# The token mixers of a hybrid diffusion trunk: linear attention laid between the projection's pages, and the other three mixers run for both streams in lockstep

## What is computed

```
h = RMSNorm(x) * (1 + scale1) + shift1
gq, gk, gv, gog, glr_f, glr_b, mcq, mckv, mkr, rq, rk, rv, rg, aq, ak, av = split(h @ w_in)   # 1024 x 2752
A = head_rms(bidir_recurrence(gq, gk, gv, log_sigmoid(glr @ gate_w + gate_b) / 16)) * silu(gog)
B = dense_attention(q from rms(mcq) @ w_q_up, k and v from rms(mckv) @ w_kv_up and mkr)
C = head_rms(bidir_recurrence(rq, rk, rv, fixed decay per head)) * silu(rg)
D = windowed attention of aq over ak, av with a sink logit
x = x + gate1 * concat(A, B, C, D) @ w_out
x = x + gate2 * FFN(RMSNorm(x) * (1 + scale2) + shift2)   # dense in layer 0, 2 of 8 experts in layer 1
```

## Time and profile before

| | us |
|---|---|
| median of 3 runs (lowest, highest) | 1899.84 (1897.28, 1901.28) |
| the profiled execution | 1889.91 |
| its span, first to last instruction | 1888.1 |
| TensorE busy | 1710.1, 91% |
| VectorE busy | 308.6, 16% |
| ScalarE busy | 233.8, 12% |
| GpSimd busy | 91.9, 5% |

### The profile page before, as it was taken

How to read it: one execution, slowest core, us unless ns; L and a number is a source line. 1 busy time by engine, 2 the same in 40 slices (tenths; PEclk the granted TensorE clock), 3 DMA queues, 4 the chain that set the end, 5 groups by cost and what they waited for, 6 DMA issues and landing times.

```text
span 1888.1 us, 42448 instructions
## 1 busy us (share of the span) xinstructions
PE 1710.1 (91%) x19946; PEld 1085.6 (57%) x19947; DVE 308.6 (16%) x731; ACT 233.8 (12%) x588; POOL 91.9 (5%) x150
## 2 busy tenths in 40 slices
PE   4996778999998976787999999999999999999995
PEld 1874354777767743545555565555655555555553
DVE  0105241000012042404001011010010100101102
ACT  1212221100002122112001010010010100101001
POOL 4022000200000030000000000000000000000000
PEclk7997778999998987577999999999999999999998
DMA  9753642444452545013898998999989999899880
GB/s 347 223 184 138 245 134 89 136 135 156 154 170 72 164 180 201 1 67 145 323 386 325 391 386 324 386 341 371 385 330 384 361 355 386 322 386 390 327 338 25
DMA packets 210447, 479.72 MB, mean 254 GB/s; under 512 B 8726, under 2 KB 54454, under 8 KB 203990
## 3 DMA queue, kind: packets, MB, share of 16 engines
q1 hardware_dynamic: 206876, 469.32, 68.1%
q0 software_dynamic: 3392, 7.63, 1.3%
HBM read 475.05 MB, written 1.87 MB: 253 GB/s over the span
## 4 chain that ended last, share of the span: by engine, by line
PE 88%; DVE 6%; ACT 3%; issue 2%; DMA 1%; SPq 0%; POOL 0%; DVEq 0%; POOLq 0%; ACTq 0%
PE ps L962 31%; PE ps L982 15%; PE ps L869 8%; PE ps L684 8%; PE ps L877 4%; PE ps L859 3%; PE ps L632 2%; PE ps L932 2%; PE ps L939 2%; PE ps L969 1%; PE ps L845 1%; DVE scratch L1423 1%; PE ps L826 1%; PE ps L706 1%; DMA arena<-in_w_mod 1%
## 5 line engine op out<-in xcount | busy, mean ns | idle before, releaser
L962 PE MATMUL ps<-arena,scratch 128*32 128x256 f32 x10752 | 605.4, 380 | 0.7 <-ACT scratch L1264 0.7
L962 PEld LDWEIGHTS ps<-arena,scratch 128*32 128x32 f32 x10752 | 342.5, 110 | 240.0 <-issue 21.5
L982 PE MATMUL ps<-arena,scratch 128*32 128x256 f32 x5376 | 300.5, 379 | 5.0 <-ACT scratch L1112 5.0
L982 PEld LDWEIGHTS ps<-arena,scratch 128*32 128x32 f32 x5376 | 174.0, 110 | 120.8 <-ACT scratch L1112 6.9
L1605 DVE TENSOR_TENSOR scratch<-scratch,ps 128x128 f32<-128x128 f32 x168 | 48.4, 288 | 782.6 <-ACT scratch L1273 782.6
L869 PE MATMUL ps<-hT,arena 128*128 128x256 f32 x704 | 157.1, 382 | 3.0 <-issue 3.0
L684 PE MATMUL ps<-arena,hT 128*128 128x256 f32 (+1 forms) x704 | 152.4, 380 | 6.2 <-issue 6.2
L869 PEld LDWEIGHTS ps<-hT,arena 128*128 128x128 f32 x704 | 134.9, 192 | 30.5 <-issue 13.0
L684 PEld LDWEIGHTS ps<-arena,hT 128*128 128x128 f32 x704 | 134.4, 193 | 24.4 <-issue 6.9
L1273 ACT ACTIVATE scratch<-ps 128x128 f32<-128x128 f32 x168 | 46.6, 277 | 801.9 <-PE ps L962 801.9
L877 PE MATMUL ps<-arena,scratch 128*128 128x512 f32 x176 | 79.0, 592 | 0.0
(11 more groups left out here) (296 smaller groups left out, 1022.6 us busy)
## 6 DMA issues: line engine op xcount, KB each, us to landing
arena<-in_moe_w_gate SPq DMA_DIRECT2D x112, 1024.0 KB, 8.3
arena<-in_moe_w_up SPq DMA_DIRECT2D x112, 1024.0 KB, 10.5
arena<-in_moe_w_down SPq DMA_DIRECT2D x112, 1024.0 KB, 13.8
arena<-in_w_mod SPq DMA_DIRECT2D x48, 1024.0 KB, 5.2
arena<-in_w_in SPq DMA_DIRECT2D x20, 1024.0 KB, 7.9
arena<-in_ffn_w_gate SPq DMA_DIRECT2D x11, 1024.0 KB, 5.5
arena<-in_ffn_w_up SPq DMA_DIRECT2D x11, 1024.0 KB, 8.0
arena<-in_ffn_w_down SPq DMA_DIRECT2D x11, 1024.0 KB, 5.1
```

What stands on the lines that cost most here:

```text
L962: ins = mm(ps[32 * g:32 * g + 32, 4 + i % 3, 0:256], e_h[:, kt, 32 * t:32 * t + 32], gate_up_pair(u, kt, g), start=(kt == 0), stop=(kt == ...
L982: ins = mm(y_part(q, t), e_hidT[:, g, 32 * t:32 * t + 32], arena[:, at + QUARTER * q:at + QUARTER * q + QUARTER], start=(first and t % 2 = ...
```

## The change

- `project` is split by page and by stream. `mixers_one` issues pages 0 to 3, then A for stream 0 and then for stream 1 in pieces, with a page or half a page of the projection, and steps of the modulation, between any two pieces. The transposes and the gates of A are made for both streams at once. The projection now uses PSUM banks 0 to 2 (it had 4 to 7), A uses 3 to 6.
- `mixers_two` runs C, B and D for both streams in lockstep: each step is issued for stream 0 and then for stream 1, with modulation steps between the steps (`MOD_PLAN`). Stream 0 has banks 0 to 2, stream 1 banks 3 to 6, and each has its own set of tiles.
- The second set of tiles lies in what were ring slots 6 to 8, so `SLOTS` goes from 9 to 6, and the second third's pages are mixed in between the last pages of w_in. Expert pages 6 to 8 now wait for `x_mixed` as the last five did.
- The SiLU of both gates is made for both streams in one go (`silu_gates`) and stored over the gate; the outputs overwrite `gv`, `mcq`, `rv` and `aq` instead of going to `mixed`. ACT loads one table that has both Exp and Ln at the head of each layer (`preload_act_table_set`). Several waits of DVE on its own last instruction (`link`) are gone. POOL's ropes, powers and stores are put into another order.

```diff
-SLOTS = 9
+SLOTS = 6
...
+        m = mod_pages(layer, 1)
+        pages += w_in_pages(layer, 0, 8) + m[0:2] + w_in_pages(layer, 8, 9) + m[2:3] + w_in_pages(layer, 9, 10)
+        pages += m[3:6] + w_in_pages(layer, 10, IN_PAGES) + m[6:]
+        pages += mod_pages(layer, 2)
...
+            def mixers_one(layer):
+
+                m1 = 3 * layer + 1
+                for i in range(4):
+                    project(layer, i)
+                gla_turn(layer)
+                project(layer, 4)
+                gla_gates(layer)
+                project(layer, 5)
+                gla_sums(layer, 0)
+                project(layer, 6)
+                gla_scores(layer, 0, 0)
+                project(layer, 7, (0,))
+                mod_steps(m1, 0, 1)
+                gla_scores(layer, 0, 1)
+                project(layer, 7, (1,))
+                mod_steps(m1, 1, 2)
+                gla_out(layer, 0)
+                project(layer, 8, (0,))
+                mod_steps(m1, 2, 3)
+                gla_sums(layer, 1)
+                project(layer, 8, (1,))
+                project(layer, 9, (0,))
+                mod_steps(m1, 3, 5)
+                gla_scores(layer, 1, 0)
+                project(layer, 9, (1,))
+                mod_steps(m1, 5, 6)
+                gla_scores(layer, 1, 1)
+                project(layer, 10, (0,))
+                mod_steps(m1, 6, 7)
+                gla_out(layer, 1)
+                project(layer, 10, (1,))
+                mod_steps(m1, 7, KT + 1)
+
+            def mixers_two(layer):
+
+                for s in range(NS):
+                    ret_turn(layer, s)
+                    mla_turn(layer, s)
+                mod_turn(3 * layer + 1)
+                for s in range(NS):
+                    ret_scores(layer, s)
+                mod_fill(layer, "ret_scores")
...
+                for kind in range(2):
+                    for s in range(NS):
+                        attention_turn(layer, s, kind)
+                    mod_fill(layer, f"turn{kind}")
+                    for s in range(NS):
+                        attention_scores(layer, s, kind)
+                    if kind == 0 and layer + 1 < L:
+                        mod_turn(3 * layer + 2)
+                    mod_fill(layer, f"scores{kind}")
+                    for s in range(NS):
+                        attention_p_turn(layer, s, kind)
+                    mod_fill(layer, f"p_turn{kind}")
+                    for s in range(NS):
+                        attention_out(layer, s, kind)
+                    mod_fill(layer, f"out{kind}")
...
+                if layer + 1 < L:
+                    MOD_PLAN.append({"ret_scores": [(2, 0, 2)], "ret_out": [(2, 2, 4)], "kv_up": [(2, 4, 6)],
+                                     "q_up": [(2, 6, KT + 1)], "p_turn0": [(3, 0, 2)], "out0": [(3, 2, 4)],
+                                     "turn1": [(3, 4, 6)], "scores1": [(3, 6, KT + 1)]})
+                else:
+                    MOD_PLAN.append({"ret_out": [(2, 0, 1)], "kv_up": [(2, 1, 2)], "q_up": [(2, 2, 3)], "turn0": [(2, 3, 4)],
+                                     "scores0": [(2, 4, 5)], "p_turn0": [(2, 5, 6)], "out0": [(2, 6, 7)],
+                                     "turn1": [(2, 7, 8)], "scores1": [(2, 8, KT + 1)]})
```

More of the change, by code:

```diff
@@ L122, in mod_pages, with w_in_pages @@
         return [("mod_bias", layer, third, 0)] + [("mod", layer, third, kt) for kt in range(KT)]
+    def w_in_pages(layer, lo, hi):
+        return [("w_in", layer, c, 0) for c in range(lo, hi)]
     for layer in range(L):
@@ new lines, in _ @@
+                rope(proj[:, 1, COL["rq"][0]:COL["rk"][1]].rearrange("p (h d) -> p h d", h=8), 8, 64).then_inc(roped, 1)
+                o_power(4 * layer)
+                pool.wait_ge(m_normed, NS * layer + 1)
+                store(io["new_cache_mla_ckv"][0, layer], m_ckv[0])
+                pool.wait_ge(g_state_kept, layer + 1)
+                for d in range(2):
+                    for h in range(H):
+                        store(io["new_state_gla"][0, layer, d, h], g_st[32 * h:32 * h + 32, d, 64 * h:64 * h + 64])
@@ L651, in spread_gate, with mod_fill @@
                 ins.then_inc(gate_spread, 1)
[L653 to L658 removed]
+            def mod_fill(layer, place):
+                for third, lo, hi in MOD_PLAN[layer].get(place, ()):
+                    mod_steps(3 * layer + third, lo, hi)
             def norm_turn(m):
@@ new lines, in q_up, with attention_of @@
+            def q_up(layer, s):
+                pe.wait_ge(o_kept, 4 * layer + 3 + s)
+                for k in range(2):
+                    ins = mm(ps[:, 3 * s, 0:384], m_qT[s][:, k, :], w_q_up[:, k, :], start=(k == 0), stop=(k == 1))
+                ins.then_inc(m_q_done, 1)
+            def attention_of(s, kind):
+                if kind == 0:
+                    return 96, H, a_q[s], [a_k[s][:, t] for t in range(1 + s)], [a_v[s][:, t] for t in range(1 + s)]
+                return (64, 2, heads(pj(s, "aq"), H), [heads(pj(s, "ak"), 2), ctx_k[:]][:1 + s],
+                        [heads(pj(s, "av"), 2), ctx_v[:]][:1 + s])
@@ new lines, in gla_pick @@
+            def gla_pick(layer, s, r):
+                n = NS * layer + s
+                dve.wait_ge(g_att_done, 2 * n + r + 1)
+                if r == 1:
+                    dve.wait_ge(g_att_kept, 2 * n + 1)
+                for j in range(4):
+                    level = 4 * r + j
+                    mask = masks[:, level, :] if level < LEVELS else ident
+                    ins = v.copy_predicated(g_att, mid(mask, H).bitcast(U32), ps[:, 3:7, P * j:P * j + P])
+                    if j < 3:
+                        link(ins)
+                ins.then_inc(g_att_kept, 1)
@@ new lines, in attention_norm @@
+            def attention_norm(layer, s, kind):
+                b = 3 * s
+                dve.wait_ge(a_out, 4 * layer + 2 * kind + s + 1)
+                total, inv = a_stat(s, A_SUM), a_stat(s, A_INV)
+                if kind == 1:
+                    link(v.tensor_tensor(total, total, a_stat(s, A_SINK_EXP), ALU.add))
+                link(v.reciprocal(inv, total))
+                v.tensor_tensor(heads(pj(s, ("mcq", "aq")[kind]), H), heads(ps[:, b + 1, 0:256], H), last(inv, 64),
+                                ALU.mult).then_inc(a_mixed, 1)
```

877 lines of the change are left out of this document (474 added, 403 removed).

## The result

The changed kernel takes 1758.28 us (median of 4 runs, 1757.42 to 1762.91), the kernel before beside it on the same chip 1898.56 us: a ratio of 0.9266, with a 95% interval of 0.9244 to 0.9288. That is 140 us faster. Two more sets of runs of the unchanged kernel gave 1757.46 and 1759.45 us; single executions of the three sets lie between 1744.30 and 1767.71 us.

A forecast was written before the change was run, and what follows sets the result against it. TensorE was taken to bound the kernel, through work, clock and waits. Gains of 49 us in layer 0, 53 in layer 1 and 3 in the out projection took 1889.9 to 1784; plus 9.9 gave 1794 us, range 1764 to 1838.

The forecast's parts named there:

- Waits: TensorE's gaps in the mixers: 4 to 10 us per layer instead of 39.5 and 47.9.
- part one: Projection with linear attention and nine modulation steps between its pages: 114 us per layer, against 142.7 before.
- Linear attention's own work: TensorE's linear attention for both streams at full clock, without modulation steps: 27 us per layer.
- The clock in part two: Other mixers in lockstep: clock 0.80 in layer 0 and 0.70 in layer 1, 72 us each with gaps.
- The bound of 0.56: Lower bound on the lockstep mixers' clock, from the last 59 us of layer 1 before, without modulation steps.
- The spread of the gates and the out projection: Out projection and gate-spreading matmuls start at a higher clock: 1.5 us gained per layer, 3 in all.
- The ring: Weight pages in 6 slots instead of 9: no page late, cost nothing.
- The step from the profile to the median: Whole kernel: 9.9 us added because the profiled execution before lay that far below its median, 1784 to 1794.
- The rival of the full clock: Clock stays full throughout the lockstep mixers: 139 us gained, 1761 us; chance 0.12.
- The slower rival: Linear attention's small matmuls pull projection pieces between them to 1.2 GHz: 1937 us; chance 0.03.
- the low clock: Clock stays at 0.56 in the lockstep mixers: 56 us gained, 1844 us; chance 0.17.
- new waits: DVE's fixed queue order for two streams brings new gaps: 1828 us if half remain, 1871 if all; chance 0.07.

The follow-up runs named there:

- late steps: Changed kernel, layer 0's modulation steps in mixers_two set singly, layer 1's nine moved later and partly between the streams; 1758.89 us, ratio 0.9256.
- its own run: Kernel before with only SLOTS set to 6 in place of 9; 1898.38 us, ratio 1.0002.
- the two parts undone together: Changed kernel with eleven projection pages in a row before linear attention, and the other mixers one stream after the other; 1880.44 us, ratio 0.9921.
- part one undone: Changed kernel with all eleven projection pages first, then linear attention with nine modulation steps between its pieces; 1823.62 us, ratio 0.9624.
- part two undone: Changed kernel with the other mixers run one stream after the other, as many modulation steps between them; 1823.61 us, ratio 0.9605.
- slow exponentials: Changed kernel with ScalarE computing each softmax's exponentials twice in layer 1, 6.4 us of delay in all; 1771.80 us, ratio 0.9337.
- single steps: Changed kernel with layer 0's 18 modulation steps in mixers_two set singly, also between the streams; 1756.27 us, ratio 0.9276.

## Why the prediction was wrong, point by point

- **Waits: right.** 4 to 10 us a layer were forecast, 5.6 and 6.0 came; part one has only the 0.9 us for page 3's copy, and every cover held.
- **Linear attention's own work: 27 us forecast, 22.8 measured** (transposes 0.65, gates 1.06, sums 6.46 + 6.57, scores 4.41, outputs 3.67, from the starts of TensorE's instructions in layer 0). Busy time times the mean clock of a stretch counts too much, since that mean runs over the waits too. That is only a part of it: weighed in stretches of 0.5 us, by TensorE's busy time in each, the clock gives 40.3 us in place of the 42.3 with the steps in it, 2 of the 4 us; where the other 2 lie stays open. There was no stretch at half clock either, for which I had put 2 us. Against these 6 us the projection took 77.6 us in pieces, not 76.2, and the nine steps 8.5, not 7.8. So part one took 109.8 us, not 114: 4.2 us in each layer, 8.4 of the miss.
- **The clock in part two: the step that failed.** I took 0.80 and 0.70 from the kinds of products and the number of wide steps. Layer 0 came out at 0.81 and 71.7 us (72 forecast), though by luck: another execution has 65.3. Layer 1 had 0.91 and 55.6 us, in another 0.81 and 62.1, where 72 was forecast: 10 to 16 us of the miss. The work in that sum was right: 47 us at full clock were forecast, and with late steps the stage had 46.0 at a clock of 1.00. Wrong was the division by 0.70. The bound of 0.56 and the mean of 0.68 that drew me down came from a stage full of waits. Serial again, it has 0.71; with its waits only filled, the stretch around it rises from 0.76 to 0.85. The waits had gone by my own sum, and I left their clock standing. The forecast's other reading, that the kinds of work matter, isn't refuted: the stretch of layer 0 at half clock with no wait in front comes behind transposes and small matmuls, and it was shorter with the wide steps set singly.
- **The spread of the gates and the out projection** were to give 3 us. The spreading takes 1.9 us (686.74 to 688.66), which is less than before, the projection 29.40 against 29.21. All that lies behind the mixers together is 1363.8 us, against 1363.0: nothing.
- **The ring: right**, by its own run.
- **The step from the profile to the median failed by 14 us.** I added the 9.9 us by which before's execution was below its median; after's was 4.6 us above its own (1762.91 and 1758.28). The executions of one kernel go with their mean granted clock (1744.30 us at 0.971, 1767.71 us at 0.955), so one execution's distance from the median says nothing of the next kernel's.

The sum of the miss, 35.7 us: 8.4 part one, 16.4 + 0.3 part two, less 3.8 behind the mixers, is 21.3, and with 14.5 for the median 35.8. The rival of the full clock, 1761 us, has the time, but not by its own working. It carries the same 9.9 us, so for the profiled execution it says 1751, and that took 1762.91. Its 61 us for part two of layer 0 were nowhere reached, and the clock was full throughout in neither stage of any profile of the changed kernel. Its 55 us for layer 1 came, at 55.6. Its reason, that TensorE is never idle for long, is borne out by the fills, but isn't the whole: the clock also fell with no wait. It was given 0.12 because the steps in layer 1 are single; in two of the three profiles they held the full clock up to the last softmax, in the third not.

The slower rival is clearly refuted: the pieces of the projection take 3.72 us, and part one's clock is 0.98. So is the low clock, and so are new waits. The Trainium skill (TensorE: Matmul & The Clock Gate, Part 4: PE-mode transpose) says that the full clock doesn't engage for transposes, which don't count as work in the same way; the small matmuls that the forecast put beside them are not in that sentence. The trace agrees in part: in the second profile the 23 transposes at the start of part two of layer 0, behind a wide step, took 0.27 us each (the first 0.30), which is 2.4 GHz. So transposes do run at the full clock, for 2.5 us here. But in the first profile the clock fell 3.5 us after the last of the same 23, and in the third 4.3 us after it, with no wait between, which fits that they don't count; whether it was they, and whether they alone would bring the clock back, no run here tried.

**What stays open.** What decides, in one execution, whether a stage of the same code with the same waits takes 6.5 us more was not found, nor what makes the clock fall in the midst of work: no run moved the transposes or put wide work between them. Nor were the 8 us by which the two parts undone together cost less than singly; and narrow fills differ from wide ones also in their weights (128 columns against 2), which was not taken apart.

## What to carry to other kernels

A wait of TensorE costs more than its length. Span against span of the profiled executions, each us of wait here went with 1.3 to 1.9 us of time: 127.0 us for 77.0 of waits in the whole change, 53.3 for 39.7 with part one undone, 61.2 for 32.6 with part two undone, 10.2 for 6.0 with the slow exponentials. The medians differ by somewhat more (140.3, 65.3, 65.3 and 13.5 us), and each profile scatters by some 6 us a stage. These are sums over many waits, in kernels that differ in their order too, and not the price of a single one. When waits are forecast to go, the low clock of their stage must not be carried over: take the clock of a stage that is full, and keep the old one as the bound. Nor does the full clock follow from having no waits: part two of layer 0 lost 6.4 us in three of five profiles to a fall in the midst of work. Where a wait can't be removed, useful wide work in front of it is worth its length and some clock, and even useless work gained 32 us of 1898.

## What the runs showed of the hardware

Filling TensorE's waits with products of zeros, 512 columns wide, makes a kernel faster by 1.7%. Products of 64 columns do so too, by 1.1%, but after a wait of 4.4 us TensorE worked for 16 us at 1.2 GHz without a break where they stood, and for 27 us where there were more of them; with wide ones it was at 2.4 GHz again 5.4 us after the wait.

The clock also falls with no wait. In six of the eight profiles of the changed kernel and its close variants (other steps, slow exponentials) TensorE's granted clock went from 1.00 to 0.50 between 166.1 and 168.4 us, after more than 80 us without a pause, behind 27 transposes and a few other instructions, and stayed there for 13.7 us in three of them and 6.8 us in the three with single steps. The granted clock of one stage varies between executions of one kernel, 0.81 or 0.90 and 0.81 or 0.91 here, which is 6 us each time; a difference of that size in one profile means nothing until medians bear it out.
